# Stick-breaking attention: the units of neighbouring head pairs are interleaved, so that each large unit stands between small ones

## The reference, cut to what matters

```python
def stick_breaking_attention(q, k, v):
    lp, d = q.shape[2], q.shape[3]
    scale = d ** -0.5
    outs = []
    for blk in range(lp // Q_BLOCK):
        q0, q1 = blk * Q_BLOCK, (blk + 1) * Q_BLOCK
        z = jnp.einsum('bhtd,bhsd->bhts', q[:, :, q0:q1], k[:, :, :q1]).astype(jnp.float32) * scale
        strict = jnp.arange(q1)[None, :] < jnp.arange(q0, q1)[:, None]
        log_1m = jnp.where(strict, jax.nn.log_sigmoid(-z), 0.0)
        csum = jnp.cumsum(log_1m, axis=-1)
        log_a = jax.nn.log_sigmoid(z) + csum[..., -1:] - csum
        a = jnp.where(strict, jnp.exp(log_a), 0.0)
        outs.append(jnp.einsum('bhts,bhsd->bhtd', a.astype(v.dtype), v[:, :, :q1]))
    return jnp.concatenate(outs, axis=2)
```

## Time and profile before

| what | value |
|---|---|
| median of three runs | 2575.2 us (2575.04 to 2575.85) |
| the profiled execution: its own time | 2576.58 us |
| the profiled execution: its span | 2574.9 us |
| PE busy | 2537.3 us, 99% |
| DVE, ACT, POOL busy | 50%, 36%, 39% |
| mean granted TensorE clock | 0.997 |
| the stick-breaking stage on PE | from about 523 to 605 us of the span |

### The profile page before, as it was taken

One profiled execution on the slowest core, in us unless ns is written; L12 is line 12 of the kernel. 1 busy time (PEld: TensorE's weight loads), 2 busy tenths in 40 slices (PEclk: granted clock), 3 DMA queues, 4 the chain that ended last, 5 costly groups with the idle time before them and its releaser, 6 DMA issues.

```text
span 2574.9 us, 34915 instructions
## 1 busy us (share of the span) xinstructions
PE 2537.3 (99%) x13348; PEld 2116.4 (82%) x13348; DVE 1281.6 (50%) x1387; ACT 935.7 (36%) x1324; POOL 998.8 (39%) x443
## 2 busy tenths in 40 slices
PE   9999999999999999999999999999999899999999
PEld 8999999966777788888777678888887678888887
DVE  4434114267445644421397666663455845666313
ACT  4222224275334342222456332222245543222222
POOL 4444344302223344435333344444443024444443
PEclk9999999999999999999999999999999999999999
DMA  4222333201112322233322122222234112222322
GB/s 165 90 90 82 96 92 115 82 20 50 58 58 73 114 96 94 97 98 96 101 93 73 66 99 98 98 97 95 94 123 123 42 50 98 95 93 97 107 98 83
DMA packets 72178, 230.86 MB, mean 90 GB/s; under 512 B 9297, under 2 KB 9553, under 8 KB 72082
## 3 DMA queue, kind: packets, MB, share of 16 engines
q1 hardware_dynamic: 63360, 215.22, 25.2%
q10 hardware_dynamic: 8722, 14.31, 1.8%
HBM read 220.58 MB, written 5.24 MB: 88 GB/s over the span
## 4 chain that ended last, share of the span: by engine, by line
PE 91%; DVE 6%; ACT 1%; issue 1%; DMA 0%; ACTq 0%; SPq 0%; DVEq 0%
PE PS L301 27%; PE PS L302 27%; PE PS L303 27%; PE PS L2945 1%; DVE acc L516 1%; PE PS L1428 1%; PE PS L1782 1%; DVE mt L1971 1%; DVE sq L508 1%; PE PS L2928 0%; PE PS L2962 0%; PE PS L1809 0%; PE PS L1412 0%; PE PS L2425 0%; DVE mixl L1975 0%
## 5 line engine op out<-in xcount | busy, mean ns | idle before, releaser
L296 POOL TENSOR_TENSOR wlo<-wraw,whi 128x1024 fp32r<-128x1024 f32 (+2 forms) x422 | 991.8, 2353 | 1515.0 <-ACT whi L289 1514.4
L301 PE MATMUL PS<-xh,whi 128*128 128x512 f32 (+2 forms) x2504 | 890.1, 355 | 8.0 <-DVE gates_a L1879 2.2
L303 PE MATMUL PS<-xh,wlo 128*128 128x512 f32 (+2 forms) x2504 | 878.7, 351 | 0.0
L302 PE MATMUL PS<-xl,whi 128*128 128x512 f32 (+2 forms) x2504 | 878.6, 351 | 0.0
L289 ACT ACTIVATE whi<-wraw 128x1024 fp32r<-128x1024 f32 (+2 forms) x422 | 426.3, 1011 | 834.6 <-PE PS L303 819.1
L301 PEld LDWEIGHTS PS<-xh,whi 128*128 128x128 f32 (+1 forms) x2504 | 470.8, 188 | 77.3 <-issue 10.3
L303 PEld LDWEIGHTS PS<-xh,wlo 128*128 128x128 f32 (+1 forms) x2504 | 471.3, 188 | 63.1
L302 PEld LDWEIGHTS PS<-xl,whi 128*128 128x128 f32 (+1 forms) x2504 | 471.2, 188 | 60.1 <-issue 1.4
L301 PE MATMUL PS<-hid2h,whi 128*128 128x512 f32 x560 | 218.0, 389 | 0.0
L302 PE MATMUL PS<-hid2l,whi 128*128 128x512 f32 x560 | 217.9, 389 | 0.0
L303 PE MATMUL PS<-hid2h,wlo 128*128 128x512 f32 x560 | 217.8, 389 | 0.0
(11 more groups left out here) (454 smaller groups left out, 3280.4 us busy)
## 6 DMA issues: line engine op xcount, KB each, us to landing
wraw<-w_up_dram SPq DMA_DIRECT2D x96, 512.0 KB, 3.2
wraw<-w_dn_dram SPq DMA_DIRECT2D x48, 512.0 KB, 3.2
wraw<-w_f1gu_dram SPq DMA_DIRECT2D x44, 512.0 KB, 3.2
wraw<-w_f2gu_dram SPq DMA_DIRECT2D x44, 512.0 KB, 3.2
wraw<-w_hyin_dram SPq DMA_DIRECT2D x24, 512.0 KB, 3.2
wraw<-w_win_dram SPq DMA_DIRECT2D x18, 512.0 KB, 3.2
wraw<-w_gate_dram SPq DMA_DIRECT2D x16, 512.0 KB, 3.2
wraw<-w_pg_dram SPq DMA_DIRECT2D x16, 512.0 KB, 3.2
```

The source lines that it names most:

```text
L296: pool.tensor_tensor(wlo[:, s, 0:size], wraw[:, s, 0:size], whi[:, s, 0:size].bitcast(F32), ALU.subtract).then_inc(lo_done.s, 1)
L301: pe.matmul(out_, whi[:, s, a:b], xhi, start=start, stop=False, skip_group_check=True)
L302: pe.matmul(out_, whi[:, s, a:b], xlo, start=False, stop=False, skip_group_check=True)
L303: return pe.matmul(out_, wlo[:, s, a:b], xhi, start=False, stop=stop, skip_group_check=True)
```

## The change

It gives the units another order. Before: (0,3) (0,2) (0,1) (0,0) (0,4), then the same for pairs 1, 2 and 3. After: (0,3) (0,2) (0,1), then for p = 0, 1, 2 the five units (p+1,3) (p,0) (p+1,2) (p,4) (p+1,1), and (3,0) (3,4) at the end. The waits that were written with 5 p now look up the place of (p, 4) in the list, and a pair's `y_out` follows the end of that pair: before at u = 6, 11, 16 on ACT and 7, 12, 17 on DVE, now at u = 8, 13, 18 and 9, 14, 19. The work attached to fixed u stays at its u. No instruction is added or removed, and no shape changes.

```diff
-            units = [(p, j) for p in range(4) for j in (3, 2, 1, 0, 4)]
+            units = [(0, 3), (0, 2), (0, 1)]
+            for p in range(3):
+                units += [(p + 1, 3), (p, 0), (p + 1, 2), (p, 4), (p + 1, 1)]
+            units += [(3, 0), (3, 4)]
             NU = len(units)
+            last = [units.index((p, 4)) for p in range(4)]
...
                     if j in (2, 3):
                         if p >= 2:
-                            dve.wait_ge(*arg_done(5 * (p - 1)))
+                            dve.wait_ge(*arg_done(last[p - 2] + 1))
                     elif p >= 1:
-                        dve.wait_ge(*arg_done(5 * p))
+                        dve.wait_ge(*arg_done(last[p - 1] + 1))
...
-                    if u % 5 == 2 and u >= 5:
-                        y_out(u // 5 - 1)
+                    if u - 3 in last:
+                        y_out(last.index(u - 3))
...
                 def y_out(pair):
-                    act.wait_ge(*pv_done(5 * pair + 5))
+                    act.wait_ge(*pv_done(last[pair] + 1))
...
-                    if u % 5 == 1 and u >= 5:
-                        y_out(u // 5 - 1)
+                    if u - 2 in last:
+                        y_out(last.index(u - 2))
```

## The result

The changed kernel takes 2580.26 us, the median of 12 runs (2576.18 to 2585.23). The kernel before takes 2575.11 us (12 runs, 2573.29 to 2576.32). The ratio is 1.0022, with a 95% interval of 1.0014 to 1.0029. So the change costs about 5.2 us of 2575. That is 0.26 us beyond the upper end of the range, and more than twice the forecast cost of 2.4 us. The runs also spread more: 9.1 us from lowest to highest, against 3.0 before.

The account below looks back on a forecast made before the run. PE, busy 99% of the span, was taken as the bound. Waits of 7.5 us after against 5.1 before cost 2.4 us: 2575.2 + 2.4 = 2577.6 us, range 2575.4 to 2580.0.

Parts of the forecast that it names:

- The waits at the large units: PE waits for the softplus ahead of (0,0), (1,0), (2,0), (3,0): 1.75, 1.82, 1.38, 0.24 us after the change.
- 17.89: PE's work for one head pair, summed from start-to-start distances of its scores, `sums` and `pv`: 17.89 us.
- the chain: From scores of (p,0): |z|, exp, ln on ACT, softplus on DVE, before `sums` may begin; 5.96 us with nothing put in.
- The y place: At `pv` of (3,3), PE waits 1.2 us for pair 1's y low part, behind three rope products; 1.9 in all.
- echo: Delay of `sums` of (3,2) after the `pv` of (3,3) wait, its softplus queued behind the y low part; 0.7 us.
- T: Start of `sums` of (2,0), from which the times up to the end of `sums` of (3,2) are counted.
- The sum of the waits: All PE waits of the stage: 7.5 us after against 5.1 before, so the change costs 2.4 us.
- the start up to (0, 0): Stage start: 0.37 us wait at `sums` of (0,1), then 1.75 lost ahead of (0,0), where 0.82 was lost before.
- the 0.3 subtracted for the low part of three (p, 1) units: Three (p,1) units each save a wait of about 0.1 us for their low part, taking 7.8 to 7.5.
- The `split` wait: `split` of (p+1,1) waits for `sums` of (p,4): hidden with 1 us to spare; rival that it shows, 2580.6, 2 in 100.
- the next stage: The next stage is driven from this one's end, so all the delay of 2.4 us is passed on.
- The clock: Granted clock stays 1.00 in the stage; rival, it falls at (1,0) or (2,0), up to 3.4 us, 2581.0, 6 in 100.

Follow-up runs that it names:

- the filled kernel with 32 columns: Changed order plus seven zero products of 32 stationary columns ahead of `sums` of (0,0), (1,0), (2,0): 2579.75 us, ratio 1.0020.
- the rope products later: Changed order, three rope products moved on DVE from u = 14 to u = 16: 2578.24 us; with the 32-column zero products too, 2577.18 us.
- the nine later runs: The changed kernel measured again without any edit: 2581.25 us, ratio 1.0027 to before.
- the first filling: Changed order plus eight zero-tile products (128 columns by 384) ahead of `sums` of (0,0), (1,0), (2,0), one more ACT copy: 2581.30 us.
- small units behind: Kernel before, reordered to (p,1) (p,0) (p+1,3) (p+1,2) (p,4): 2576.45 us, ratio 1.0005.
- the first pair alone: Changed order only up to (1,4), pairs 2 and 3 ordered as before: 2575.74 us, ratio 1.0002.

## Why the prediction was wrong

**The waits at the large units: right.** From the filled kernel with 32 columns, whose clock was 1.00, (0, 0) to (1, 0) are 561.55 - 541.93 = 19.62 us. The prediction's terms give 17.89 + 1.82 = 19.71. From (1, 0) to (2, 0) it is 19.71 by the 512-column rows, against 17.89 + 0.36 + 1.38 = 19.63. The idle rows of 1.73, 1.85 and 1.47 us stand where 1.6, 1.7 and 1.2 were forecast. In the changed kernel nothing is printed ahead of (3, 0), and 0.34 ahead of (0, 1), for 0.37. The cause, that the long (p, 1) accumulation no longer covers the chain, is shown from both sides: with it put back ahead of the large unit the stage is 82.01, and with each chain longer the order of before loses the same length four times over.

**The y place: right, and 0.4 too small.** `pv` of (3, 3) waited 1.20 us for the forecast 1.2. Wait and echo cost 2.26 us, and 1.9 was taken. In the filled kernel `sums` of (3, 2) ended at T + 7.17, for a forecast T + 6.9, and with the rope products later at T + 4.99, as forecast without the wait. The three DVE steps of (3, 2) took 1.94 us, as the estimate of 1.9 had it, though the rows that the prediction names give only about 1.6 by the number of columns.

**The sum of the waits: too small by 0.9.** 3.3 us were measured and 2.4 forecast. Beside the y place, the start up to (0, 0) was 0.2 longer than its terms gave (3.51 more than before, where 2.03 of moved work and 0.37 + 1.75 - 0.82 of waits make 3.33). And of the 0.3 subtracted for the low part of three (p, 1) units these distances show at most 0.1, from (0, 0) to (1, 0). By the waits alone the median would be 2575.2 + 3.3 = 2578.5, in the range.

**The `split` wait and the next stage: right.** No PE idle above 0.25 us stands at the low part of a (p, 1) unit. From the 512-column row of (3, 0) to the next stage are 6.95 us in the filled kernel and 6.94 before, so all of the delay is passed on.

**The clock: this step failed.** It is the term that the sum put at nothing. The prediction let it stand at 1.00 because the 0.85 and 1.27 us gaps had left it alone, gave its fall 6 in 100, and put the point from which it decides at the 2.15 us of the start. Each of the three profiles of this order with open gaps (the changed kernel twice, and with the rope products later) has two or three half-clock stretches of 3.4 us. Two profiles with the gaps filled, and a third with the rope products later too, have none. A stretch cost between nothing, where it ran into a wait that was there anyway, and 1.6 us; together 1.5 to 4.2 us an execution. So the threshold was wrong, being read from the single gap of 2.15. The kernel before has a gap of 1.48 us as well, at 795.89. It left the clock alone in both profiles of that kernel, and the same gap brought it down in five of the 12 others.

The fall was also priced as one event, when the order makes four gaps in a row that each can bring it. The Trainium skill (page "TensorE: Matmul & The Clock Gate", section "HAM oscillation — how this bites in real kernels") tells of such a repeated fall, where every turn of a loop has its gap and pays anew; its gaps are longer than any of this stage. These traces agree that it repeats, and show it behind gaps of 1.2 to 1.85 us. They do not show it at every turn: a given gap brought it in one execution and not in the next. The advice that the prediction names (the same page of the Trainium skill, section "Why this matters for your kernels") is for longer gaps too. By its letter the clock would have stayed up here, and the measurement decides against it.

**How the median divides is only partly settled.** It is 5.2 us over before (6.5 in the nine later runs). The waits are 3.3 of them by the stage. The remaining 1.9 (or 3.2) fit the half clock, but no median shows it. Taken as differences to before, the first filling stands no lower than the unfilled kernel, the second 0.5 to 1.8 us lower, and with the rope products later the filled one 1.4 us lower, none of it clear of the intervals. All runs list a mean granted clock (in steps of 0.001, so only means over many runs say anything), from which 2 x (1 - clock) x 2575 us gives the time at half level: about 20 us in the 21 runs of the changed kernel, 13.0 to 13.6 in the runs of before, 15.5 with the 32-column filling and 13.6 with the rope products later as well. Some 7 us more at half speed are worth at most 3.5. But the filled kernels also stand 1.1 to 3.3 us further over before than their stage does, and small units behind 1.6, with no half clock in their stages. Something outside the stage, or in executions that were not profiled, adds about 1 us to several of these kernels. What it is was not found. The stretch at 795 to 800 us is not it, as far as the profiles show a cost.

**What decides whether a gap brings the clock down stays open.** Not its length alone: ahead of (2, 0) the clock fell as a gap of 1.46 us ended in one execution and stayed at 1.00 for 7 us behind one of 1.47 in the other, and 1.94 and 2.36 us in the order of before did not bring it down. Nor the instructions around it: the first pair alone has the same gap of 1.73 and did not fall, and the gap near 795 us, the same in every kernel, brought it down in five profiles of 14. At (0, 0) it fell in three profiles of three, so the chance need not be the same at every place.

## What to carry to other kernels

Before interleaving units, add up for each long dependent chain what the other engine has to do between its start and its use: the order that alternates large with small may take away just the long piece of work that covered it. On a full PE, a gap of the length seen here can cost more than its length: leave room in the range for up to 1.6 us of a half-clock stretch behind each, unless a wait follows that hides it. And a single gap that left the clock alone is no proof that the next will. When a kernel's runs spread wider than those of the one before, look at the clock in windows of 1 us before looking for a wait.

## What the runs showed of the hardware

- Half clock inside a dense stage came in pieces of 3.4 us, behind gaps of 1.2 to 1.85 us, and began between 0 and 2.2 us after the end of a gap. Gaps of 1.94 to 2.36 us in another order were followed by none in their profiles. Over the same products, the high and low triangle products of 512 columns started 0.84 us apart for 0.47 at full clock.
- The same gap of 1.47 to 1.48 us, among the same instructions near 795 us in every kernel, was followed by 3.4 us at half clock in five profiles of 14.
- With seven products of 32 stationary columns of zeros, 384 columns wide, in each of three gaps no half clock was left in the stage (two profiles), as with eight of 128 columns (one profile).
- The length of half clock near the start of the program varied between executions, and the start of the stage with it. Over the 14 profiles the stage began at 518.73 and 519.88 us with none, at 520.00 to 522.13 with 3.4 us (six profiles), and at 522.73 to 523.39 with 6.8 (six profiles; the last has one more copy ahead of the stage). The spread of 4.7 us is more than most edits here moved. The start of a stage is to be subtracted before two spans are compared.
